# Layer 1's projection works on un-normed rows and scales what it takes from PSUM; its k and v product stands last in each tile, and weight loads ahead of its own

## The reference

```python
def rmsnorm(x, g):
    x32 = x.astype(F32)
    y = x32 * lax.rsqrt(jnp.mean(x32 * x32, axis=-1, keepdims=True) + EPS)
    return (y * g.astype(F32)).astype(x.dtype)

def swa_sink_attention(u, positions, w_qkv, b_qkv, sinks, w_o, b_o):
    q, k, v = jnp.split(u @ w_qkv + b_qkv, [1024, 1152], axis=-1)
    ...
    q = partial_rotary(q, cos, sin)
    k = partial_rotary(k, cos, sin)
    ...

# for each layer
u = rmsnorm(h, mix_norm[layer])
h = h + mixer(u, ...)
u = rmsnorm(h, ffn_norm[layer])
h = h + hierarchical_moe(u, ...)
```

## Time and profile before

| | |
|---|---|
| median of 3 runs | 2370.56 us (2370.04 to 2372.09) |
| profiled execution | 2367.21 us, span 2365.3 us |
| PE busy | 2111.9 us (89%) |
| PE weight loads | 1733.3 us (73%) |
| DVE busy | 1615.5 us (68%) |
| ACT busy | 1330.3 us (56%) |
| POOL busy | 233.6 us (10%) |
| mean granted clock of TensorE | 0.939 |
| layer 1's projection, first load issued to last take | 1217.6 to 1368.8 us of the span |

### The profile page before, as it was taken

One profiled execution on the slowest core, in us unless ns is written; L12 is line 12 of the kernel. 1 busy time (PEld: TensorE's weight loads), 2 busy tenths in 40 slices (PEclk: granted clock), 3 DMA queues, 4 the chain that ended last, 5 costly groups with the idle time before them and its releaser, 6 DMA issues. The chain is left out here.

```text
span 2365.3 us, 29800 instructions
## 1 busy us (share of the span) xinstructions
PE 2111.9 (89%) x10507; PEld 1733.3 (73%) x10507; DVE 1615.5 (68%) x1917; ACT 1330.3 (56%) x1632; POOL 233.6 (10%) x251
## 2 busy tenths in 40 slices
PE   6979997998599999999949978889679999999990
PEld 4768875776488888888837867778568888888870
DVE  3552233665688888888834367726678988988975
ACT  4322424443487887887833246622168788788762
POOL 1100000000011111111113410000011111111100
PEclk9989997999799999999979978989889999999995
DMA  3112222113499999999943020000379999999966
GB/s 123 36 44 82 70 63 71 55 54 161 145 351 387 389 386 386 379 377 383 384 176 104 1 81 1 1 9 28 142 250 377 382 378 387 387 387 389 385 256 227
DMA packets 122159, 512.96 MB, mean 217 GB/s; under 512 B 27149, under 2 KB 28250, under 8 KB 87258
## 3 DMA queue, kind: packets, MB, share of 16 engines
q1 hardware_dynamic: 102490, 474.09, 53.4%
q0 software_dynamic: 18432, 33.60, 3.7%
q10 hardware_dynamic: 1152, 4.19, 0.5%
HBM read 495.03 MB, written 50.33 MB: 231 GB/s over the span
## 5 line engine op out<-in xcount | busy, mean ns | idle before, releaser
L438 DVE TENSOR_TENSOR exp_w_lo<-ring_raw,exp_w_hi 128x2048 fp32r<-128x2048 f32 x384 | 865.0, 2288 | 81.3 <-ACT exp_w_hi L372 81.3
L372 ACT ACTIVATE exp_w_hi<-ring_raw 128x2048 fp32r<-128x2048 f32 x384 | 729.2, 1918 | 165.8 <-PE exp_up_out L321 65.3
L321 PE MATMUL exp_gate_out<-exp_w_hi,exp_x_hi 128*128 128x512 f32 x512 | 207.3, 405 | 5.9 <-DVE exp_x_lo L442 5.9
L321 PE MATMUL exp_y_out<-exp_w_hi,exp_hid_hi 128*128 128x512 f32 x512 | 205.4, 401 | 3.8 <-DVE exp_hid_lo L453 3.8
L321 PE MATMUL exp_gate_out<-exp_w_lo,exp_x_hi 128*128 128x512 f32 x512 | 202.5, 395 | 0.0
L321 PE MATMUL exp_gate_out<-exp_w_hi,exp_x_lo 128*128 128x512 f32 x512 | 202.4, 395 | 0.0
L321 PE MATMUL exp_y_out<-exp_w_hi,exp_hid_lo 128*128 128x512 f32 x512 | 201.4, 393 | 0.0
L321 PE MATMUL exp_y_out<-exp_w_lo,exp_hid_hi 128*128 128x512 f32 x512 | 200.9, 392 | 0.0
L321 PE MATMUL exp_up_out<-exp_w_hi,exp_x_lo 128*128 128x512 f32 x512 | 199.4, 389 | 0.0
L321 PE MATMUL exp_up_out<-exp_w_hi,exp_x_hi 128*128 128x512 f32 x512 | 199.2, 389 | 0.0
L321 PE MATMUL exp_up_out<-exp_w_lo,exp_x_hi 128*128 128x512 f32 x512 | 199.2, 389 | 0.0
(11 more groups left out here) (430 smaller groups left out, 3990.7 us busy)
## 6 DMA issues: line engine op xcount, KB each, us to landing
ring_raw<-in_expert_w_gate_dram SPq DMA_DIRECT2D x128, 1024.0 KB, 9.8
ring_raw<-in_expert_w_up_dram SPq DMA_DIRECT2D x128, 1024.0 KB, 10.1
ring_raw<-in_expert_w_down_dram SPq DMA_DIRECT2D x128, 1024.0 KB, 10.2
l0w_raw<-in_ab_w_in_dram SPq DMA_DIRECT2D x48, 256.0 KB, 2.8
l_q<-y_rows SPq DMA_DIRECT2D x8, 1024.0 KB, 5.1
finish_y<-y_rows SPq DMA_DIRECT2D x8, 1024.0 KB, 9.5
base_h<-in_x_dram ACTq DMA_DIRECT2D x8, 512.0 KB, 6.6
gate_rows<-l0w_stage SPq DMA_DIRECT2D x16, 256.0 KB, 2.0
```

Source lines behind the costliest of these rows:

```text
L321: last = nc.tensor.matmul(out, x[:, k0 + k], w[:, k, cols], start=(first and k == 0 and t == 0), stop=(last_unit and k == K - 1 and t == 2))
L372: nc.scalar.activation(split[split_slot(unit)][0][:], raw[raw_slot(unit)][:], ACT.Copy).then_inc(hi_ready, 1)
L438: nc.vector.tensor_tensor(lo[:], raw[raw_slot(unit)][:], hi[:].bitcast(F32), ALU.subtract).then_inc(lo_ready[split_slot(unit)], 1)
```

## The change

Several things change together, all in layer 1's first part. PE transposes h[:, t] itself, so rows_of, its semaphores and the normed rows go. The scale comes in at take_qkv: each of its two operations becomes a scalar_tensor_tensor, times scale, plus bias. In project(t) the k and v product moves from the front to the end, and qkv_made is raised by it. u_cols gets two buffers, its copy waits for lo_made, and u_low waits for hi_made alone. SP issues all four weight transfers ahead of w_kv and y(1). ACT and DVE work on the weights in another order at the start.

```diff
-                sp.dma_start(w_kv[:], w_in[:, :, n_q:]).then_inc(s["kv_ready"], 16)
-                for u in range(3):
+                for u in range(4):
                     load_w(w_in, u)
+                sp.dma_start(w_kv[:], w_in[:, :, n_q:]).then_inc(s["kv_ready"], 16)
                 load_y(1)
-                load_w(w_in, 3)
...
                     rotate(t)
                     if t == 0:
                         pool.wait_ge(s["bias_o_ready"], 16)
-                    pool.wait_ge(s["rows_made"], t + 1)
+                    pool.wait_ge(s["u_turned"], t + 1)
+                    pool.wait_ge(s["rooted"], t + 1)
                     g.tensor_tensor(h[:, t], h[:, t], bias_o[:], ALU.add).then_inc(s["h_biased"], 1)
...
                 def turn_u(t):
-                    pe.wait_ge(s["rows_made"], t + 1)
+                    pe.wait_ge(s["combined"], t + 1)
                     if t >= 1:
-                        pe.wait_ge(s["hi_made"], t)
                         pe.wait_ge(s["f_made"], t)
-                        pe.wait_ge(s["lo_made"], t)
                     for k in range(8):
-                        last = nc.tensor.transpose(turned[:, k], rows[t % 2][:, k * P:(k + 1) * P], c["ident"][:])
+                        last = nc.tensor.transpose(turned[:, k], h[:, t, k * P:(k + 1) * P], c["ident"][:])
...
                 def project(t):
                     j = t % 2
-                    if t == 0:
-                        pe.wait_ge(s["kv_scaled"], 1)
-                    pe.wait_ge(s["f_made"], t + 1)
                     if t >= 2:
                         pe.wait_ge(s["taken"], 2 * t - 2)
                         pe.wait_ge(s["keys_made"], t - 1)
-                    for k in range(8):
-                        last = nc.tensor.matmul(wide[j][:, n_q:n_qk + n_kv], u_cols[:, k], w_kv[:, k], start=(k == 0), stop=(k == 7))
-                    last.then_inc(s["kv_made"], 1)
                     pe.wait_ge(s["lo_made"], t + 1)
                     split_product(scores[j], u_hi[j], u_lo[j], 1 if t == 0 else None, range(4))
                     if t >= 1:
                         turn_k(t - 1, k_turn[(t - 1) % 2])
...
-                    split_product(scores[j], u_hi[j], u_lo[j], 1 if t == 0 else None, range(4, 8)).then_inc(s["qkv_made"], 1)
+                    split_product(scores[j], u_hi[j], u_lo[j], 1 if t == 0 else None, range(4, 8))
+                    if t == 0:
+                        pe.wait_ge(s["kv_scaled"], 1)
+                    pe.wait_ge(s["f_made"], t + 1)
+                    for k in range(8):
+                        last = nc.tensor.matmul(wide[j][:, n_q:n_qk + n_kv], u_cols[j][:, k], w_kv[:, k], start=(k == 0), stop=(k == 7))
+                    last.then_inc(s["qkv_made"], 1)
...
-                def rows_of(t):
-                    act.wait_ge(s["scaled"], t + 1)
-                    a.activation(rows[t % 2], h[:, t], ACT.Copy, scale=scale[:, t:t + 1]).then_inc(s["rows_made"], 1)
...
-                    if t >= 1:
-                        act.wait_ge(s["kv_made"], t)
-                    a.activation(u_cols, turned[:], ACT.Copy).then_inc(s["f_made"], 1)
+
+                def u_copy(t):
+                    act.wait_ge(s["lo_made"], t + 1)
+                    a.activation(u_cols[t % 2], turned[:], ACT.Copy).then_inc(s["f_made"], 1)
...
                 def u_low(t):
-                    dve.wait_ge(s["f_made"], t + 1)
+                    dve.wait_ge(s["hi_made"], t + 1)
...
-                    v.tensor_tensor(q[:, t], wide[t % 2][:, 0:n_qk], row_a[:, 0:n_qk], ALU.add).then_inc(s["taken"], 1)
-                    v.tensor_tensor(vals[:, t], wide[t % 2][:, n_qk:n_qk + n_kv], row_a[:, n_qk:], ALU.add).then_inc(s["taken"], 1)
+                    v.scalar_tensor_tensor(q[:, t], wide[t % 2][:, 0:n_qk], scale[:, t:t + 1], row_a[:, 0:n_qk], ALU.mult, ALU.add).then_inc(s["taken"], 1)
+                    v.scalar_tensor_tensor(vals[:, t], wide[t % 2][:, n_qk:n_qk + n_kv], scale[:, t:t + 1], row_a[:, n_qk:], ALU.mult, ALU.add)\
+                        .then_inc(s["taken"], 1)
```

More of the change, by code:

```diff
@@ L1881, in layer1 @@
         y = [q[:, 4 + 2 * j:6 + 2 * j].rearrange("p t n -> p (t n)")[:, 0:2048].rearrange("p (k d) -> p k d", k=2) for j in range(2)]
-        rows, u_cols = [work[0][:], work[1][:]], chunks(work[2][:])
+        squares, u_cols = work[0][:], [chunks(work[1 + j][:]) for j in range(2)]
         u_hi, u_lo = ([chunks(split_work[first + 2 * j][:]) for j in range(2)] for first in (3, 4))
@@ L1902, in layer1 @@
         names = ("pos_ready", "bias_ready", "bias_o_ready", "kv_ready", "router_ready", "gain_ready", "reduced", "sines", "tables",
-                 "combined", "rooted", "scaled", "rows_made", "u_turned", "hi_made", "f_made", "lo_made", "kv_scaled", "w_hi_made", "w_split",
-                 "kv_made", "qkv_made", "taken", "cleared", "rotated", "h_biased", "k_turned", "keys_made", "q_turned", "q_copied",
+                 "combined", "rooted", "u_turned", "hi_made", "f_made", "lo_made", "kv_scaled", "w_hi_made", "w_split",
+                 "qkv_made", "taken", "cleared", "rotated", "h_biased", "k_turned", "keys_made", "q_turned", "q_copied",
                  "scored", "masked_made", "tops_made", "prob_made", "prob_turned", "prob_copied", "out_ready", "out_taken", "q_next",
@@ L1932, in _ @@
                 load_y(0)
+                for u in range(4):
+                    load_w(w_in, u)
                 sp.dma_start(w_kv[:], w_in[:, :, n_q:]).then_inc(s["kv_ready"], 16)
-                for u in range(3):
-                    load_w(w_in, u)
                 load_y(1)
-                load_w(w_in, 3)
                 sp.dma_start(row_a[:], broadcast_row(A["swa_b_qkv"][0], P)).then_inc(s["bias_ready"], 16)
@@ L2034, in project @@
                         turn_first_queries()
-                    split_product(scores[j], u_hi[j], u_lo[j], 1 if t == 0 else None, range(4, 8)).then_inc(s["qkv_made"], 1)
+                    split_product(scores[j], u_hi[j], u_lo[j], 1 if t == 0 else None, range(4, 8))
[5 more added lines that the diff above has]
+                    last.then_inc(s["qkv_made"], 1)
                 def turn_first_queries():
-                    pe.wait_ge(s["hi_made"], T)
                     pe.wait_ge(s["f_made"], T)
-                    pe.wait_ge(s["lo_made"], T)
                     for k in range(8):
@@ L2210, in root_of @@
                     act.wait_ge(s["combined"], t + 1)
-                    if t >= 2:
-                        act.wait_ge(s["u_turned"], t - 1)
-                    a.activation(rows[t % 2], h[:, t], ACT.Square, accum_out=c["sums"][:, t:t + 1])
+                    a.activation(squares, h[:, t], ACT.Square, accum_out=c["sums"][:, t:t + 1])
                     act.drain()
                     a.activation(root[:, t:t + 1], c["sums"][:, t:t + 1], ACT.Sqrt, bias=c["eps"][:], scale=1.0 / 1024).then_inc(s["rooted"], 1)
-                def rows_of(t):
-                    act.wait_ge(s["scaled"], t + 1)
-                    a.activation(rows[t % 2], h[:, t], ACT.Copy, scale=scale[:, t:t + 1]).then_inc(s["rows_made"], 1)
                 def u_high(t):
@@ L2279, in _ @@
                 act.sem_inc(s["sines"], 1)
-                root_of(0)
-                rows_of(0)
+                w_high(0)
                 u_high(0)
-                w_high(0)
                 w_high(1)
-                root_of(1)
-                rows_of(1)
+                u_copy(0)
                 w_high(2)
                 w_high(3)
[L2290 to L2293, removed]
+                root_of(0)
+                root_of(1)
+                for t in range(1, T):
                     u_high(t)
+                    u_copy(t)
+                    if t + 1 < T:
+                        root_of(t + 1)
                 act.wait_ge(s["q_turned"], 1)
@@ L2355, in scale_of @@
                     dve.wait_ge(s["rooted"], t + 1)
-                    v.reciprocal(scale[:, t:t + 1], root[:, t:t + 1]).then_inc(s["scaled"], 1)
+                    v.reciprocal(scale[:, t:t + 1], root[:, t:t + 1])
+                    dve.drain()
                 def w_low(u):
@@ L2477, in _ @@
                 combine(0)
-                scale_of(0)
+                w_low(0)
                 u_low(0)
-                w_low(0)
                 w_low(1)
-                combine(1)
-                scale_of(1)
                 w_low(2)
                 w_low(3)
+                combine(1)
                 combine(2)
@@ L2491, in _ @@
                         u_low(t + 1)
-                    if t + 2 < T:
-                        scale_of(t + 2)
+                    scale_of(t)
                     take_qkv(t)
```

## The result

| | before | after |
|---|---|---|
| median (20 runs each) | 2367.14 us | 2378.30 us |
| ratio of after to before, 95% interval | | 1.0044 (1.0035 to 1.0053) |
| span of the profiled execution | 2365.3 us | 2374.8 us |
| load of y(0) to tile 1's first matmul | 41.15 us | 40.56 us |
| load of y(0) to the last take | 150.8 us | 158.6 us |

The change makes the kernel slower by 0.44%, some 10 us, clear of the noise. The two kernels reach the first load of the stage at slightly different times (1217.99 and 1214.55), before anything has changed, so lengths within the stage are counted from that load.

What follows compares the result with a forecast made beforehand. PE was taken to bound layer 1's projection, with waits only at start-up. Terms -1.2 + 7.0 + 0.3 gave +6.1 us, 2376.6 us from the 2370.56 median; the range was 2370 to 2380.

Steps and rivals of the forecast that it cites:

- two collisions of POOL and DVE: Layer 1's projection: POOL's w_kv scaling holds up DVE at start-up; POOL's rotation beside DVE's combine makes turn_k late.
- chain to combine(1): Start-up: weights, w_low and POOL's scaling in sequence, 3.4 us of it collision, end combine(1) at 1246.2.
- Rival B: Start-up: scaling w_kv costs DVE nothing, gain 4.6 us, total +2.7, 2373.3 us; chance 0.25.
- The gain: Start-up: tile 1 starts at 1257.9 against 1259.14, 1.2 us gained.
- The price of leaving the collision out: Start-up bounds: without the collision tile 1 starts at 1254.5, and at full clock too at 1252.9.
- Rival E: Start-up: no gain, as POOL's scaling or late weights cost 2 to 3 us more; +8 to +9, 2379; chance 0.12.
- The cost of the scaled take: Last take only: scalar_tensor_tensor and a later start behind the k and v product, 0.3 us together.
- The term of 7.0 us: Steady part: PE waits 1.4 us at turn_k for POOL's rotation in five tiles, 7.0 us lost.
- Rival C: Steady part: rotation is over in time, turn_k not late; -0.9 us, 2369.7 (2366.3 with B's start); chance 0.08.
- Rival D: Steady part: stalls bring the clock down, each losing up to another 1.7 us; +14.6, 2385; chance 0.05.
- the stage's shift: Attention, output projection and experts follow in series, so the projection's shift reaches the kernel's end one for one.

Runs made afterwards that it cites:

- e2: Changed kernel, with POOL's scaling of w_kv made to wait for combine(1); median 2365.1 us, ratio to the kernel before 0.9982.
- e3: Changed kernel, with DVE's combine(t+3) made to wait until rotate(t) is through; median 2365.1 us, ratio to the kernel before 0.9986.
- e4: Changed kernel, with turn_k moved behind the split product's second half and POOL's scaling of w_kv waiting for combine(1); median 2360.8 us, ratio to before 0.9975.
- e6: Changed kernel, with SP's loads in their old order (w_kv, w0, w1, w2, y(1), w3); median 2379.8 us, ratio to the kernel before 1.0057.

## Why the prediction was right, and where it was short

**Direction and mechanisms: right.** Slower was forecast with 0.59, by two collisions of POOL and DVE, and both are in the profile at their places. Within the stage 6.1 us were forecast and 7.8 measured.

**Start-up.** The chain to combine(1) came out to the tenth: forecast 1246.2 with the load at 1217.99, 28.2 us behind it; measured 1242.76 with the load at 1214.55, 28.2. The w_low operation beside POOL was forecast at 4.7 us and took 4.63. Rival B (no collision) is refuted by that row and by e2. The gain was 0.6 us, not 1.2, because the clock came back later: from combine(1) to the k and v product PE took 9.1 us, where 8.4 had been reckoned with the loss of the earlier trace rows. The granted clock was 0.50 from 1242.8 to 1244.8 and 0.54 from there to 1248.5. PE stood 5.5 us and not the 6.6 forecast, since tile 0's first half ended later, 22.8 us after the load instead of 21.6; combine(1) sets tile 1's start, so this had no price. The price of leaving the collision out was put at 3.4 us, and another 1.6 if the clock stayed up; e2 measured 5.7. Rival E (a start-up 2 to 3 us worse than forecast) is refuted: it was 0.6 worse.

**Steady part.** Late in tiles 1 to 5 and in time in 6 and 7, as forecast. The term was sized 1.4 us each, 7.0 in all, and measured some 1.57 in four periods and 1.91 in the fifth, 8.2 in all. Of the 0.17 in each, 0.07 are a later release: turn_k starts 6.92 us after the take where 6.85 had been reckoned, for take and vals, now with the scale, start POOL 1.76 us after the take instead of 1.63. Another 0.05 are the step from 1.45 down to 1.4, and 0.05 come behind turn_k. In tile 2's rotation another 0.34 us are lost to a gap of POOL's ("issue", ahead of its third operation), which no term had. The cost of the scaled take had been put at the last tile alone, as part of 0.3 us, which measured 0.25; it also stood on the path of every tile where turn_k was late, since the cover was gone. The term of 7.0 us was the one most undersized in the stage, though by little. Rival C is refuted by the idle rows; its own condition, combine no longer meeting the rotation, is what e3 makes true: there the sum was 150.6 us, where rival C had put the projection 0.9 us under the kernel before. Rival D is refuted by the granted clock of 1.00 from the first take to the last.

**Behind the stage.** The prediction carried the stage's shift one for one to the end. The projection accounts for 7.8 of some 10 us. In the profiles attention is some 5 us longer, at a lower granted clock, and what comes behind it is the same within 1 us in all five profiles of the two kernels (807.3 to 808.1 us to the end of the span). The time before the first load of the stage varies by 3.6 us (1214.6 to 1218.2), so the split of the medians is no finer than that. The prediction put this change behind the stage at nothing and had no term for attention. It also started from a median of three runs, 2370.56 us, 3.4 above that of twenty, and this made up for most of what was missing: as a difference 6.1 us were forecast, and 11.2 measured by the medians, 10.4 by the ratio. That the time came within 1.7 us of the forecast 2376.6 is luck to that extent.

**What stays open:** what makes attention's granted clock come out lower behind the changed kernel's projection. It isn't the stalls at turn_k, which e2 has too, at 184 to 188 us, and e4 has not, at 192 to 194, and not the transposes of un-normed rows, which all kernels here but the one before have. No run here separates it further.

## What to carry to other kernels

When work is moved on the engine that sets the pace, ask what it covered: the k and v product at the front of a tile was 3.26 us of cover for a chain over DVE and POOL that needed some 1.6 of them. When a load is moved, follow what it releases: a POOL operation with SBUF inputs that starts among DVE operations with two SBUF inputs holds the next of them up for nearly its whole length (3.35 us for one of 3.60), and one wait that puts it beside another stretch of DVE's work can be worth more than what the change gained at the start (here 5.7 us and 0.6). And where a stage's clock differs from profile to profile, compare the stage that was changed, from its own first instruction.

## What the runs showed of the hardware

- A DVE scalar_tensor_tensor with two SBUF inputs takes 1.28 us alone and 4.63 us when a POOL tensor_tensor of 3.60 us is waiting when its turn comes; even without a drain between the DVE operations POOL gets in. Where POOL was first, as with the scaling in e2, DVE's combine took 3.44 us. In the other direction POOL's 0.49 us operations take 1.47 us. The Trainium skill's "SBUF — State Buffer", section "Who interferes with whom", describes it as an exclusive hold for a whole instruction, and the rows agree.
- The scale in the take costs 0.06 us in each of its two operations (1.42 us for 1.36, 0.34 for 0.28), with PSUM as one input.
- An idle time of 2.06 us left PE at full clock (eight transposes in 1.10 us), one of 5.51 us did not (1.97 us), nor did one of 4.35 us in e6 (1.97 us).
- Two profiles of the same kernel differ by 3.7 us (e2) in one stage of 190 us at the same instructions.
